# Two blocks at 256 tokens: another order of the attention slots, forget sums in one matmul, and transposed hidden units in both feed-forwards

## The chip, the cores and the metric

The kernel runs on one NeuronCore of a Trainium2 chip. The metric is the device time of one execution in microseconds (us); lower is better. Engines are named as in the profile: PE is TensorE, PEld its weight loads, DVE VectorE, ACT ScalarE, POOL GpSimd and SP SyncE.

## The reference

Two transformer blocks run one after the other on x (256 tokens, 1,024 channels, float32).

```python
# first block
u = rms_norm(h, g_mix); z = u @ w_in
y_a = sliding_window_attention(q_a, k_a, v_a, sinks) @ w_br_swa   # 8 heads of 64, 2 key heads
y_b = forgetting_attention(q_b, k_b, v_b, f_b + b_forget) @ w_br_fox  # scores + c[q] - c[k], c = cumsum(log_sigmoid(f))
h = h + (gates[0] * y_a + gates[1] * y_b) @ w_mix_out
h = h + square(relu(rms_norm(h, g_mlp) @ w_ff1)) @ w_ff2          # 4,096 hidden units
h = h + sigmoid(rms_norm(h, g_ple) @ w_ple_gate) * (p @ w_ple_proj)
y = rms_norm(h, g_final)
# second block, on y, modulated by silu(c) @ w_ada + b_ada
# selected-key attention (8 heads), retention (4 heads), gates, w_out, then
x = x + gate2 * ((silu(h2 @ w_ffn_gate) * (h2 @ w_ffn_up)) @ w_ffn_down)   # 2,816 hidden units
out = rms_norm(x, final_norm_w)
```

## The kernel before

**Weights as units.** Every weight matrix comes through one stream of units of 128 x 1,024 values (two contraction tiles of 128 by 512 columns, or for the down projections one contraction tile by two halves of 512). SP loads a unit into one of the slots of `raw`. ACT copies it to `w_hi` as float32r (a rounded upper half), and DVE subtracts to get `w_lo` (the lower half). `w_hi` and `w_lo` have 4 slots (`SPLIT`), so ACT may write unit u only when PE has used unit u - 4, and both engines run 3 units ahead of PE (`AHEAD`; 2 in the gated feed-forward). A product is three matmuls (`mm3`, L1460): hi x hi, hi x lo, lo x hi.

**A unit on PE.** `unit_pair` (L1466) keeps 128 rows of the activations stationary and moves 512 weight columns: 2 contraction tiles x 2 tiles of rows x 3 = 12 matmuls of 512 columns, with a weight load each. `unit_wide` (L1487) does the same for the down projections.

**The attention slots.** Loop `for n in range(20)` in each engine's program. In slot n, PE does the unit of gate weights 20 + n, the scores of head n, the transposes of the probabilities of head n - 2 (`head_pt`) and the output product of head n - 3 (`head_pv`). Heads 0 to 7 are the sliding-window ones, 8 to 15 the forgetting ones. For a forgetting head each of the two score matmuls is followed by one that adds the cumulative sums (`cum`, 256 columns, picked by the table `pick`, L1601). The other two engines have their order written out:

```python
# ACT, slot n                           # DVE, slot n
split_to(u + AHEAD)                     split_to(20 + n + AHEAD)
(gates' tanh where n % 4 == 3)          head_min(n)
head_exp(n)                             head_norm(n - 1)
head_pt(n - 2)                          head_out_lo(n // 2 - 2)   # n even
head_out_hi(n // 2 - 2)   # n even
```

`head_min` (L965) takes the scores from PSUM and leaves them and their minima in SBUF; `head_exp` (L576) needs that; `head_norm` (L975) needs the exponentials; PE's `head_pt` needs the normed probabilities; ACT's `head_pt` (L585) copies the transposed ones; `head_out_hi` (L591) and `head_out_lo` (L984) split the output of a pair of heads out of bank 7, and PE's `head_pv` of the next pair waits for `aT_lo`. The second block's selected-key attention has the same slots at q = 33 to 44 of a loop over 60 units (head q - 17), without sinks, with `head_out_hi` and `head_out_lo` both at q = 37, 39, 41 and 43.

**The squared-ReLU feed-forward.** 8 chunks of 512 hidden units. Per chunk, 4 units of w_ff1 give the hidden units in banks 0 and 1 with tokens on the partitions; ACT applies relu with the norm's rstd as scale (L688) and squares (L691); PE transposes them into banks 2 and 3 (`hidden_T`, 8 transposes, L1502); ACT and DVE split them into `xT_hi`, `xT_lo` (L696, L1113); 4 units of w_ff2 are added to banks 4 to 7 one chunk later. During this loop DVE also sums the modulation (`ada_acc`, L1134), whose weights POOL loads.

**The gated feed-forward.** 11 chunks of 256 hidden units: 4 units that hold 256 gate columns and 256 up columns (banks 0 and 1, one tile of tokens each), tanh on ACT (L862), two products on DVE (L1410, L1412), 4 transposes on PE (`ffn_T`, L1848), the split (L858, L1403), and 2 units of the down projection.

Of the kernel before, what the change touches and what calls it, by code (L numbers as in the profile page):

```python
# [60 lines left out]
def constants():  # L61
# [71 lines left out]
    "relu": "ACT: relu tiles", "squared": "ACT: squared tiles", "hid_T": "PE: banks of transposed hidden units", "hid_hi": "ACT: upper halves",  # L133
# [8 lines left out]
    "ffn_tanh": "ACT: tanh(gate / 2)", "ffn_silu": "DVE: twice silu", "ffn_hid": "DVE: twice the hidden units", "ffn_T": "PE: transposed",  # L142
    "ffn_hi": "ACT: upper halves", "ffn_lo": "DVE: lower halves", "ffn_out": "PE: the output's banks",
# [27 lines left out]
def build(nc, x, p, g_mix, w_in, b_forget, swa_sinks, w_br_swa, w_br_fox, w_mix_out, g_mlp, w_ff1, w_ff2,  # L171
# [86 lines left out]
    with ExitStack() as ctx:  # L258
# [26 lines left out]
        cum = sb("cum", [LO_ROW + HEADS, SEQ], F32R)  # L285
# [23 lines left out]
        nr8 = sm(2)  # L309
        neg_half = sm(8).rearrange("p (k t) -> p k t", t=2)  # L310
# [217 lines left out]
        def _(act):  # L528
# [96 lines left out]
            for c in range(1, 5):  # L625
# [59 lines left out]
            def relu2(j_done):  # L685

                for t in range(TILES):
                    nc.scalar.activation(nat[:, 0, t, :], B[:, t, :], ACT.Relu, scale=rstd[:, 1, t:t + 1]).then_inc(sem("relu"), 1)  # L688
                act.wait_ge(sem("relu"), j_done)
                for t in range(TILES):  # L690
                    nc.scalar.activation(nat[:, 1, t, :], nat[:, 0, t, :], ACT.Square).then_inc(sem("squared"), 1)  # L691

            def hidden_hi(banks=(0, 1)):
                for i in banks:
                    b = 2 + i
                    nc.scalar.activation(xT_hi[:, 2 * i:2 * i + 2, :], B[:, b, :].rearrange("p (k n) -> p k n", k=2),  # L696
                                         ACT.Copy).then_inc(sem("hid_hi"), 1)
# [3 lines left out]
            act.wait_ge(sem("rstd_done"), 2)  # L701
            act.wait_ge(units_used, U_FF + 4)
            relu2(2)
            act.wait_ge(sem("hid_T"), 2)
            hidden_hi()
            with act.Fori(1, FF_CHUNKS) as j:
# [85 lines left out]
            for q in range(60):  # L792
# [27 lines left out]
                if 13 <= q < 21:  # L820
                    i = q - 13
                    act.wait_ge(sem("index_done"), i + 1)
                    if i >= 2:
                        act.wait_ge(sem("index_sum"), i - 1)
                    nc.scalar.activation(prob[:, i % 2, :], B[:, 4 + i % 2, 0:KEYS], ACT.Relu).then_inc(sem("index_relu"), 1)
                if 33 <= q < 41:
                    head_exp(q - 17, False)
                if 35 <= q < 43:
                    head_pt(q - 19)
# [38 lines left out]
            ffn_hi(0, 1)
            with act.Fori(0, (FN_CHUNKS - 1) // 2) as i:
# [23 lines left out]
        def _(dve):  # L893
# [134 lines left out]
            for k in (1, 2, 3):  # L1028
# [7 lines left out]
                if k == 2:  # L1036
                    dve.wait_ge(sem("cum_hi"), 1)
                    low = slice(LO_ROW, LO_ROW + HEADS)
                    nc.vector.tensor_tensor(cum[low, :], B[low, 7, 0:SEQ], cum[low, :].bitcast(F32), ALU.subtract).then_inc(sem("cum_lo"), 1)

            for n in range(2 * HEADS + 4):
                split_to(20 + n + AHEAD)
                if n < HEADS:
# [66 lines left out]
            def hidden_lo(i, count):  # L1110
                    b = 2 + i
                    dve.wait_ge(sem("hid_hi"), count)
                    nc.vector.tensor_tensor(xT_lo[:, 2 * i:2 * i + 2, :], B[:, b, :].rearrange("p (k n) -> p k n", k=2),  # L1113
# [27 lines left out]
            split_to(U_FFE + 3 + AHEAD)  # L1141
            dve.wait_ge(units_used, U_FFE + 4)
            for t in range(TILES):
                add_h(t, 0, 4 + t)
            for t in range(TILES):
                add_h(t, 1, 6 + t)
# [114 lines left out]
            for q in range(60):  # L1261
# [40 lines left out]
                if 33 <= q < 41:  # L1302
                    if q == 33:
                        dve.wait_ge(sem("selected"), 1)
                    head_min(q - 17, selected)
                if 34 <= q < 42:
                    head_norm(q - 18, False)
                if q in (37, 39, 41, 43):
# [603 lines left out]
```

## Time and profile before

| | |
|---|---|
| median of 3 runs | 876.91 us (876.29 to 877.5) |
| the profiled execution | 877.04 us, of which the span is 875.4 us |
| PE busy | 845.4 us (97%), 3,999 matmuls |
| DVE / ACT / POOL busy | 588.8 (67%) / 443.8 (51%) / 52.4 us (6%) |
| chain that ended last | PE 91%, ACT 3%, DVE 2%, issue 2%, DMA 1% |
| mean granted TensorE clock | 0.991 of full |

Busy time is the sum of the instructions' durations without overlap; matmul records overlap each other, so the pace of PE is read from start to start. A slot or a chunk is found by the line numbers. In a timeline, a row "x3" is three instructions merged, and a bracket at its end tells how long the engine sat idle before it and what it waited for.

### The profile page before, as it was taken

Reading aid. Unit: us, or ns where it says so; the run is one execution under the profiler, and the core shown is the slowest. Engines: PE = TensorE matmul, PEld = TensorE weight load, DVE = VectorE, ACT = ScalarE, POOL = GpSimd, SP = SyncE. Lnnn points to the kernel's source line nnn. Section 1 sums busy time; section 2 is a strip of 40 time slices with the busy share of each in tenths; the row PEclk is TensorE's granted clock in tenths of the full one; section 3 lists DMA queues with packets and bytes.
Section 4 is the critical chain, followed back from the end, with each engine's and each line's share of the span. In section 5 each row is a group of like instructions: output and inputs, shape, how many; then the busy total and the mean of one; then the engine's idle time right before and its main releaser. Section 6 shows DMA issues by size and latency. Waiting matters only on the chain.

```text
span 875.4 us, 11575 instructions
## 1 busy us (share of the span) xinstructions
PE 845.4 (97%) x3999; PEld 704.5 (80%) x3999; DVE 588.8 (67%) x902; ACT 443.8 (51%) x693; POOL 52.4 (6%) x67
## 2 busy tenths in 40 slices
PE   6999999999999999997999999999998999999996
PEld 5888888887888888875988887888887788888885
DVE  4756665867788777877766986656675746545555
ACT  6546665456444445567544436544543535434442
POOL 4000000102000000201100000011000000000000
PEclk9999999999999999999899999999999999999999
DMA  8854334688989898541565564545545365665641
GB/s 278 286 170 141 106 118 140 180 336 314 343 318 320 328 323 320 186 146 25 181 203 153 151 194 149 148 143 171 188 114 166 131 213 155 213 189 164 200 136 48
DMA packets 87621, 170.42 MB, mean 195 GB/s; under 512 B 8176, under 2 KB 32984, under 8 KB 87584
## 3 DMA queue, kind: packets, MB, share of 16 engines
q1 hardware_dynamic: 82272, 142.63, 50.7%
q0 software_dynamic: 5312, 27.30, 9.1%
q8 instruction: 22, 0.36, 0.2%
q14 instruction: 15, 0.12, 0.0%
HBM read 168.84 MB, written 1.05 MB: 194 GB/s over the span
## 4 chain that ended last, share of the span: by engine, by line
PE 91%; ACT 3%; DVE 2%; issue 2%; DMA 1%; POOL 0%; SPq 0%; DVEq 0%; POOLq 0%; ACTq 0%
PE B L1462 27%; PE B L1464 27%; PE B L1463 27%; PE B L1502 3%; PE B L1731 1%; ACT w_hi L536 1%; PE B L1521 1%; DMA raw<-in_w_in_dram 1%; PE B L1510 1%; PE B L1599 1%; ACT Z L579 1%; ACT junk L572 1%; PE B L1767 1%; DVE Z L971 1%; PE B L1848 1%
## 5 line engine op out<-in xcount | busy, mean ns | idle before, releaser
L1462 PE MATMUL B<-w_hi,xT_hi 128*128 128x512 f32 (+2 forms) x760 | 301.5, 397 | 1.3 <-DVE w_lo L908 1.3
L1464 PE MATMUL B<-w_hi,xT_lo 128*128 128x512 f32 (+2 forms) x760 | 294.2, 387 | 0.0
L1463 PE MATMUL B<-w_lo,xT_hi 128*128 128x512 f32 (+2 forms) x760 | 293.9, 387 | 0.0
L908 DVE TENSOR_TENSOR w_lo<-raw,w_hi 128x1024 fp32r<-128x1024 f32 (+2 forms) x156 | 186.9, 1210 | 87.8 <-ACT w_hi L536 86.4
L536 ACT ACTIVATE w_hi<-raw 128x1024 fp32r<-128x1024 f32 (+2 forms) x156 | 158.7, 1029 | 94.7 <-PE B L1464 87.9
L1464 PEld LDWEIGHTS B<-w_hi,xT_lo 128*128 128x128 f32 x760 | 144.1, 190 | 29.0
L1462 PEld LDWEIGHTS B<-w_hi,xT_hi 128*128 128x128 f32 x760 | 144.2, 190 | 28.8 <-issue 2.2
L1463 PEld LDWEIGHTS B<-w_lo,xT_hi 128*128 128x128 f32 x760 | 144.2, 190 | 26.7
L1462 PE MATMUL B<-w_hi,sT_hi 128*128 128x512 f32 x328 | 129.6, 395 | 0.0
L1464 PE MATMUL B<-w_hi,sT_lo 128*128 128x512 f32 x328 | 128.0, 390 | 0.0
L1463 PE MATMUL B<-w_lo,sT_hi 128*128 128x512 f32 x328 | 127.7, 389 | 0.0
L1422 DVE TENSOR_TENSOR w_lo<-raw,w_hi 128x1024 fp32r<-128x1024 f32 x60 | 72.2, 1220 | 37.5 <-ACT w_hi L875 37.5
L711 ACT ACTIVATE w_hi<-raw 128x1024 fp32r<-128x1024 f32 x56 | 58.5, 1057 | 53.0 <-PE B L1464 53.0
L1126 DVE TENSOR_TENSOR w_lo<-raw,w_hi 128x1024 fp32r<-128x1024 f32 x56 | 67.3, 1222 | 25.9 <-ACT w_hi L711 24.9
L875 ACT ACTIVATE w_hi<-raw 128x1024 fp32r<-128x1024 f32 x60 | 62.3, 1057 | 42.8 <-PE B L1464 42.8
L1464 PEld LDWEIGHTS B<-w_hi,sT_lo 128*128 128x128 f32 x328 | 61.6, 188 | 13.2
L1463 PEld LDWEIGHTS B<-w_lo,sT_hi 128*128 128x128 f32 x328 | 61.7, 188 | 12.3
L1462 PEld LDWEIGHTS B<-w_hi,sT_hi 128*128 128x128 f32 x328 | 61.6, 188 | 12.3
L1134 DVE SCALAR_TENSOR_TENSOR Z<-Z,small 128x1536 f32<-128x1536 f32 x28 | 50.7, 1811 | 1.1 <-DMA Z<-in_w_ada_dram 1.1
L579 ACT ACTIVATE Z<-Z,small 128x128 f32<-128x128 f32 (+1 forms) x48 | 21.5, 448 | 43.1 <-DVE small L971 43.1
L1410 DVE SCALAR_TENSOR_TENSOR Z<-Z,B 128x512 f32<-128x512 f32 x11 | 7.6, 688 | 40.6 <-ACT Z L862 40.6
L862 ACT ACTIVATE Z<-B 128x512 f32<-128x512 f32 x11 | 6.6, 600 | 48.3 <-PE B L1464 48.3
(205 smaller groups left out, 698.8 us busy)
## 6 DMA issues: line engine op xcount, KB each, us to landing
raw<-in_w_in_dram SPq DMA_DIRECT2D x88, 512.0 KB, 3.7
raw<-in_w_ff_dram SPq DMA_DIRECT2D x64, 512.0 KB, 6.2
Z<-in_w_ada_dram POOLq DMA_DIRECT2D x32, 768.0 KB, 7.6
raw<-in_w_ffn_gate_dram SPq DMA_DIRECT2D x44, 256.0 KB, 3.5
raw<-in_w_ffn_up_dram SPq DMA_DIRECT2D x44, 256.0 KB, 4.1
raw<-in_w_ffn_down_dram SPq DMA_DIRECT2D x20, 512.0 KB, 4.3
raw<-in_w_mix_out_dram SPq DMA_DIRECT2D x8, 512.0 KB, 3.7
raw<-in_w_ple_gate_dram SPq DMA_DIRECT2D x8, 512.0 KB, 4.1
```

What stands on the lines that cost most here:

```text
L536: nc.scalar.activation(w_hi[:, u % SPLIT, :, 0:n], raw[:, st.slot[u], :, 0:n], ACT.Copy).then_inc(hi_done, 1)
L579: last = nc.scalar.activation(prob[:, n % 2, k0:k1], prob[:, n % 2, k0:k1], ACT.Exp, scale=-1.0, bias=rmin[:, n, t:t + 1], accum_out=psum_ ...
L711: nc.scalar.activation(w_hi[:, u % SPLIT, :, :], raw[:, st.slot[u], :, :], ACT.Copy).then_inc(hi_done, 1)
L875: nc.scalar.activation(w_hi[:, u % SPLIT, :, :], raw[:, st.slot[u], :, :], ACT.Copy).then_inc(hi_done, 1)
L908: nc.vector.tensor_tensor(w_lo[:, u % SPLIT, :, 0:n], raw[:, st.slot[u], :, 0:n], w_hi[:, u % SPLIT, :, 0:n].bitcast(F32), ALU.subtract).t ...
L1126: nc.vector.tensor_tensor(w_lo[:, u % SPLIT, :, :], raw[:, st.slot[u], :, :], w_hi[:, u % SPLIT, :, :].bitcast(F32), ALU.subtract).then_in ...
L1134: nc.vector.scalar_tensor_tensor(ada_acc[:, 1536 * q:1536 * (q + 1)], ada_raw[:, q, :], silu_now, ada_acc[:, 1536 * q:1536 * (q + 1)], ALU ...
L1422: nc.vector.tensor_tensor(w_lo[:, u % SPLIT, :, :], raw[:, st.slot[u], :, :], w_hi[:, u % SPLIT, :, :].bitcast(F32), ALU.subtract).then_in ...
L1462: nc.tensor.matmul(bank, xh, wh, start=start, stop=False)
L1463: nc.tensor.matmul(bank, xh, wl, start=False, stop=False)
L1464: return nc.tensor.matmul(bank, xl, wh, start=False, stop=stop)
L1502: m = nc.tensor.transpose(B[:, b, kk * SEQ + t * P:kk * SEQ + (t + 1) * P], src(t, 2 * i + kk), ident)
```

## The change

In both attentions ACT copies the transposed probabilities of head n - 2 before the exponentials of head n. DVE norms head n - 1 before it takes the minima of head n, and splits a pair's output at slot 2m + 5 instead of 2m + 4, between the norm and the minima. In the forgetting heads the cumulative sums are laid out over the 384 key columns and added with one matmul of 384 columns ahead of the two score matmuls.

In both feed-forwards the first product has the weights stationary and the activations moving (`unit_T`): 4 groups of 128 hidden units x 2 contraction tiles x 3 = 24 matmuls of 256 columns, so the hidden units come out on the partitions and `hidden_T` and `ffn_T` are gone. Bank 0 holds the first 256 hidden units of the unit's 512, bank 1 the others. The norm's rstd is applied squared when the output is added (`rstd2`), since it is now along the free axis. ACT starts on bank 0 at a new signal (`first_bank`), half way through the last unit.

```diff
-                    nc.scalar.activation(cum[:, :], B[0:LO_ROW + HEADS, 7, 0:SEQ], ACT.Copy).then_inc(sem("cum_hi"), 1)
+                    nc.scalar.activation(cum[:, :], B[0:LO_ROW + HEADS, 7, 0:KEYS], ACT.Copy).then_inc(sem("cum_hi"), 1)
@@ ACT, attention slots (and in the same way at q = 33 to 44)
+                if 0 <= n - 2 < 16:
+                    head_pt(n - 2)
                 if n < 16:
                     head_exp(n, n < HEADS)
-                if 0 <= n - 2 < 16:
-                    head_pt(n - 2)
                 if 4 <= n < 20 and n % 2 == 0:
                     head_out_hi(n // 2 - 2, n // 2 - 2)
@@ ACT, squared-ReLU feed-forward
+            def relu2(j_done, chunks):
+                for b in range(2):
+                    if b == 0:
+                        act.wait_ge(sem("first_bank"), chunks)
+                    else:
+                        act.wait_ge(units_used, j_done)
+                    nc.scalar.activation(nat[:, 0, b, :], B[:, b, :], ACT.Relu).then_inc(sem("relu"), 1)
@@
-                act.wait_ge(units_used, j * 8 + (U_FFL - 4))
-                relu2(j * 2 + 2)
+                relu2(j * 8 + (U_FFL - 4), j + 1)
+                act.wait_ge(sem("hid_lo"), j * 2)
+                square(j * 2 + 2)
                 for r in range(7, 7 + AHEAD):
                     loop_split(r)
-                act.wait_ge(sem("hid_T"), j * 2 + 1)
-                hidden_hi((0,))
+                hidden_hi(0, j * 2 + 1)
@@ ACT, gated feed-forward
-                    act.wait_ge(units_used, i * 12 + (U_FNL + 6 * half + 4))
+                    act.wait_ge(sem("first_bank"), i * 2 + (FF_CHUNKS + half + 2))
                     ffn_tanh(1 - half)
@@ DVE, attention slots (and in the same way at q = 33 to 44)
                 split_to(20 + n + AHEAD)
+                if 0 <= n - 1 < 16:
+                    head_norm(n - 1, n - 1 < HEADS)
+                if n >= 5 and n % 2 == 1:
+                    head_out_lo((n - 5) // 2, (n - 5) // 2)
                 if n < HEADS:
                     head_min(n, distance, 2.0 ** -(n + 1), nsink[:, n:n + 1])
                 elif n < 16:
                     head_min(n, causal)
-                if 0 <= n - 1 < 16:
-                    head_norm(n - 1, n - 1 < HEADS)
-                if n >= 4 and n % 2 == 0 and n < 20:
-                    head_out_lo(n // 2 - 2, n // 2 - 2)
@@ DVE, end of the squared-ReLU feed-forward
+            dve.wait_ge(sem("rstd_done"), 2)
+            link(nc.vector.tensor_tensor(rstd2, rstd[:, 1, :], rstd[:, 1, :], ALU.mult))
@@ PE
+            def unit_T(u, xh, xl, kt0, banks, first, last, free=None):
+                s = u % SPLIT
+                for i in range(4):
+                    bank, c0 = banks[i // 2], SEQ * (i % 2)
+                    if free is not None and i % 2 == 0:
+                        pe.wait_ge(*free[i // 2])
+                    cols = slice(i * P, (i + 1) * P)
+                    for kk in range(2):
+                        o, xk, xlk = B[:, bank, c0:c0 + SEQ], xh[:, kt0 + kk, :], xl[:, kt0 + kk, :]
+                        nc.tensor.matmul(o, w_hi[:, s, kk, cols], xk, start=first and kk == 0 and i % 2 == 0, stop=False)
+                        nc.tensor.matmul(o, w_hi[:, s, kk, cols], xlk, start=False, stop=False)
+                        m = nc.tensor.matmul(o, w_lo[:, s, kk, cols], xk, start=False, stop=last and kk == 1 and i % 2 == 1)
+                    if last and i == 1:
+                        m.then_inc(sem("first_bank"), 1)
+                m.then_inc(units_used, 1)
@@
+                    if not swa:
+                        nc.tensor.matmul(B[:, 4 + n % 2, 0:KEYS], pick[:, n - HEADS, :], cum[:, :], start=True, stop=False)
                     for t, (k0, k1) in enumerate(TILE_KEYS):
-                        if not swa:
-                            m = nc.tensor.matmul(s, pick[:, n - HEADS, :], cum[:, 0:k1 - k0], start=False, stop=True)
@@
-            pe.wait_ge(sem("squared"), 2)
-            hidden_T()
             with pe.Fori(1, FF_CHUNKS) as j:
                 for r in range(4):
                     pe.wait_ge(lo_done, j * 8 + (U_FFL + r - 7))
-                    unit_pair(U_FFL + r, sT_hi, sT_lo, 2 * r, (0, 1), r == 0, r == 3, 512)
+                    unit_T(U_FFL + r, sT_hi, sT_lo, 2 * r, (0, 1), r == 0, r == 3,
+                           [(sem("relu"), j * 2 - 1), (sem("relu"), j * 2)] if r == 0 else None)
@@
-            pe.wait_ge(sem("ffn_hid"), 1)
-            ffn_T(0)
@@
-                        if e == 4:
-                            pe.wait_ge(sem("ffn_hid"), i * 2 + (half + 2))
-                            ffn_T(1 - half)
```

## Rows read from the trace of the kernel before

**Rows 1.** The page, part 1: busy time, share of the span and instructions of each engine
```profile
PE 845.4 (97%) x3999; PEld 704.5 (80%) x3999; DVE 588.8 (67%) x902; ACT 443.8 (51%) x693; POOL 52.4 (6%) x67
```

**Rows 2.** Timeline of PE, a gated chunk; columns: start us, us, engine, line, operation, out<-in, xcount
```profile
741.22 0.60 PE L1848 MATMUL B<-cst,Z 128*128 128x128 f32 x4
...
744.42 0.39 PE L1462 MATMUL B<-w_hi,xT_hi 128*128 128x512 f32 x1
...
758.03 0.60 PE L1848 MATMUL B<-cst,Z 128*128 128x128 f32 x4
```

**Rows 3.** Timeline of PE, squared-ReLU loop, two passes' transposes
```profile
220.13 1.03 PE L1502 MATMUL B<-cst,nat 128*128 128x128 f32 x8
...
242.79 1.04 PE L1502 MATMUL B<-cst,nat 128*128 128x128 f32 x8
```

**Rows 4.** Timeline of PE, 264-column matmuls of the first chunk
```profile
16.93 0.28 PE L1464 MATMUL B<-w_hi,xT_lo 128*128 128x264 f32 x1
...
19.45 0.28 PE L1464 MATMUL B<-w_hi,xT_lo 128*128 128x264 f32 x1
```

**Rows 5.** Timeline of PE, 72-column matmuls of the second w_in
```profile
431.51 0.28 PE L1462 MATMUL B<-w_hi,xT_hi 128*128 128x72 f32 x1
...
435.75 0.28 PE L1464 MATMUL B<-w_hi,xT_lo 128*128 128x72 f32 x1
```

**Rows 6.** Timeline of PE, ways into the squared-ReLU loop and into the gated loop
```profile
200.08 1.10 PE L1657 MATMUL B<-sT_hi,zero_r 128*128 128x512 f32 x4
...
203.69 0.48 PE L1462 MATMUL B<-w_hi,sT_hi 128*128 128x512 f32 x1
...
691.16 1.10 PE L1857 MATMUL B<-xT_hi,zero_r 128*128 128x512 f32 x4
...
693.87 0.48 PE L1462 MATMUL B<-w_hi,xT_hi 128*128 128x512 f32 x1
```

**Rows 7.** Windows view, 240:380: us, busy PE, PEld, DVE, ACT, POOL, PEclk, DMA, GB/s
```profile
240.00:380.00 140.00, 140.00 (x649) 116.43 (x649) 111.74 (x97) 70.93 (x87) 16.18 (x21) 1.00 0.83 293
```

**Rows 8.** Timeline of ACT, first attention; the last bracket is the idle time before and its releaser
```profile
73.77 1.04 ACT L536 ACTIVATE w_hi<-raw 128x1024 fp32r<-128x1024 f32 x1
...
90.88 0.47 ACT L589 ACTIVATE Z<-B 128x384 f32<-128x384 f32 x1
91.25 0.37 ACT L593 ACTIVATE sT_hi<-B 128x256 fp32r<-128x256 f32 x1
91.51 1.05 ACT L536 ACTIVATE w_hi<-raw 128x1024 fp32r<-128x1024 f32 x1
...
95.98 1.05 ACT L536 ACTIVATE w_hi<-raw 128x1024 fp32r<-128x1024 f32 x1
```

**Rows 9.** Timeline of DVE, the same slots
```profile
89.68 0.15 DVE L978 TENSOR_TENSOR small<-small 128x2 f32<-128x2 f32 x1
...
90.07 0.55 DVE L981 TENSOR_SCALAR Z<-Z,small 128x128 f32<-128x128 f32 x2
91.64 0.42 DVE L986 TENSOR_TENSOR sT_lo<-B,sT_hi 128x256 fp32r<-128x256 f32 x1 [1.03 <-ACT sT_hi L593]
92.59 1.23 DVE L908 TENSOR_TENSOR w_lo<-raw,w_hi 128x1024 fp32r<-128x1024 f32 x1 [0.52 <-ACT w_hi L536]
93.73 0.35 DVE L971 CUSTOM_DVE_ANT_0 Z<-B,cst,small 128x128 f32<-128x128 f32 x1
```

**Rows 10.** Timeline of ACT, selected attention, splits of weight units
```profile
523.80 1.04 ACT L536 ACTIVATE w_hi<-raw 128x1024 fp32r<-128x1024 f32 x1
...
540.31 1.05 ACT L536 ACTIVATE w_hi<-raw 128x1024 fp32r<-128x1024 f32 x1
...
544.48 1.04 ACT L536 ACTIVATE w_hi<-raw 128x1024 fp32r<-128x1024 f32 x1
```

**Rows 11.** Timeline of PE, products of heads' outputs: slot 15, and slot 7 of the second
```profile
138.57 0.60 PE L1521 MATMUL B<-Z 128*128 128x256 f32 x2
...
549.92 0.60 PE L1521 MATMUL B<-Z 128*128 128x256 f32 x2
```

More of the change, by code:

```diff
@@ L131 @@
     "gated": "DVE: branches times their gates", "mixed_done": "DVE: merged halves' tiles",
-    "relu": "ACT: relu tiles", "squared": "ACT: squared tiles", "hid_T": "PE: banks of transposed hidden units", "hid_hi": "ACT: upper halves",
+    "relu": "ACT: relu tiles", "squared": "ACT: squared tiles", "first_bank": "PE: first of the two banks of a chunk of hidden units", "hid_hi": "ACT: upper halves",
     "hid_lo": "DVE: lower halves", "pT_done": "PE: p transposed", "pT_hi": "ACT: upper half", "pT_lo": "DVE: lower half",
@@ L140 @@
     "mod_1": "DVE: columns of the first norm", "mod_2": "DVE: columns of the second norm", "gate_sum": "PE: gates' rows", "gate_b": "ACT: their copies",
-    "ffn_tanh": "ACT: tanh(gate / 2)", "ffn_silu": "DVE: twice silu", "ffn_hid": "DVE: twice the hidden units", "ffn_T": "PE: transposed",
-    "ffn_hi": "ACT: upper halves", "ffn_lo": "DVE: lower halves", "ffn_out": "PE: the output's banks",
+    "ffn_tanh": "ACT: tanh(gate / 2)", "ffn_silu": "DVE: twice silu", "ffn_hid": "DVE: twice the hidden units",     "ffn_hi": "ACT: upper halves", "ffn_lo": "DVE: lower halves", "ffn_out": "PE: the output's banks",
 }
@@ L309, in build @@
         nr8 = sm(2)
+        rstd2 = sm(2)
         neg_half = sm(8).rearrange("p (k t) -> p k t", t=2)
@@ L683, in _, with square, hidden_hi @@
             split_to(U_FF + 1 + AHEAD)
[L685 to L697, printed above, removed]
-            split_to(U_FF + 3 + AHEAD)
[L701 to L705, printed above, removed]
+            def relu2(j_done, chunks):
[5 more added lines that the diff above has]
+                    nc.scalar.activation(nat[:, 0, b, :], B[:, b, :], ACT.Relu).then_inc(sem("relu"), 1)
+            def square(count):
+                for b in range(2):
+                    act.wait_ge(sem("relu"), count - 1 + b)
+                    nc.scalar.activation(nat[:, 1, b, :], nat[:, 0, b, :], ACT.Square).then_inc(sem("squared"), 1)
+            def hidden_hi(b, count):
+                act.wait_ge(sem("squared"), count)
+                nc.scalar.activation(xT_hi[:, 2 * b:2 * b + 2, :], nat[:, 1, b, :].rearrange("p (k n) -> p k n", k=2),
+                                     ACT.Copy).then_inc(sem("hid_hi"), 1)
+            split_to(U_FF + 3 + AHEAD)
+            relu2(U_FF + 4, 1)
+            square(2)
+            hidden_hi(0, 1)
+            hidden_hi(1, 2)
             with act.Fori(1, FF_CHUNKS) as j:
@@ L1301, in _ @@
                     nc.vector.tensor_tensor(selected[:, :], work, causal, ALU.max).then_inc(sem("selected"), 1)
[L1302 to L1305, printed above, removed]
+                if q == 33:
+                    dve.wait_ge(sem("selected"), 1)
                 if 34 <= q < 42:
                     head_norm(q - 18, False)
-                if q in (37, 39, 41, 43):
-                    head_out_lo((q - 37) // 2 + 8, (q - 37) // 2)
+                if q in (38, 40, 42, 44):
+                    head_out_lo((q - 38) // 2 + 8, (q - 38) // 2)
+                if 33 <= q < 41:
+                    head_min(q - 17, selected)
                 if q in (40, 44):
@@ L1427, in _ @@
                         ffn_split(6 * half + q)
-                    ffn_hidden(1 - half, i * 2 + (half + 2))
+                    ffn_hidden(1 - half, i * 2 + (half + 2), i * 12 + (U_FNL + 6 * half + 4))
                     for q in range(4 + FFN_AHEAD, 6 + FFN_AHEAD):
@@ L1564, in _ @@
                     pe.wait_ge(sem("ones"), 1)
-                    nc.tensor.matmul(B[0:LO_ROW + HEADS, 7, 0:P], lf[:, 0, :], upper, start=True, stop=True)
-                    nc.tensor.matmul(B[0:LO_ROW + HEADS, 7, P:SEQ], lf[:, 0, :], ones, start=True, stop=False)
-                    nc.tensor.matmul(B[0:LO_ROW + HEADS, 7, P:SEQ], lf[:, 1, :], upper, start=False, stop=True).then_inc(sem("cum_done"), 1)
+                    for c0 in (0, P):
+                        nc.tensor.matmul(B[0:LO_ROW + HEADS, 7, c0:c0 + P], lf[:, 0, :], upper, start=True, stop=True)
+                    nc.tensor.matmul(B[0:LO_ROW + HEADS, 7, SEQ:KEYS], lf[:, 0, :], ones, start=True, stop=False)
+                    nc.tensor.matmul(B[0:LO_ROW + HEADS, 7, SEQ:KEYS], lf[:, 1, :], upper, start=False, stop=True).then_inc(sem("cum_done"), 1)
             for n in range(2 * HEADS + 4):
@@ L1641, in _ @@
                     transposes((2, 3), half_rows(h, 0), "wt_done")
-            def hidden_T():
-                transposes((2, 3), lambda t, k: nat[:, 1, t, k * P:(k + 1) * P], "hid_T")
             for kp in range(4):
@@ L1649, in _ @@
                 pe.wait_ge(lo_done, u + 1)
-                unit_pair(u, sT_hi, sT_lo, 2 * kp, (0, 1), kp == 0, kp == 3)
+                unit_T(u, sT_hi, sT_lo, 2 * kp, (0, 1), kp == 0, kp == 3)
                 if kp == 0:
@@ L1843, in _ @@
             normed_T((4, 5), h, 1, None)
-            def ffn_T(par):
-                for kk in range(2):
-                    for t in range(TILES):
-                        m = nc.tensor.transpose(B[:, 2 + par, kk * SEQ + t * P:kk * SEQ + (t + 1) * P],
-                                                ffn_hid[:, par, t * 256 + kk * P:t * 256 + (kk + 1) * P], ident)
-                m.then_inc(sem("ffn_T"), 1)
             for kp in range(4):
```

57 lines of the change are left out of this document (25 added, 32 removed).

## The prediction

> **What bounds the kernel.** The profiled execution took 877.04 us, 1.6 us more than its span of 875.4; the median of the runs is 876.91, so a sum made against the profiled execution is lowered by 0.13 at the end. I read the page's busy times first: PE is busy 97% of the span, DVE 67%, ACT 51% [rows 1]. The busy share of PE overstates it, because the records overlap; so I went to its timeline and took the pace from start to start. Between two sets of transposes in the gated feed-forward, 60 matmuls of 512 columns start in 13.61 us, 0.2268 us each [rows 2], without a gap. In the squared-ReLU loop the windows view shows PE busy for 140 of 140 us, with DVE at 111.7, and the DMA at 0.83 of its time [rows 7]. So in both feed-forwards the time is PE's instructions, and only what PE no longer issues counts.
>
> The attentions are different. Row by row, ACT and DVE take turns there: ACT splits a weight unit (91.51), DVE can subtract only then (92.59, after an idle time), takes the minima when that is through (93.73), ACT must have these for its exponentials, copies the transposed probabilities, and only then comes its next split (95.98) [rows 8, 9]. This ring takes 4.47 us, and 0.26 more in slots with `head_out_hi` (91.25 to 91.51). PE's waits there are small, because a slot of PE is about as long as the ring. An instruction moved into the ring therefore lengthens every slot, and one moved out shortens it, even though DVE and ACT are far from full.
>
> **The feed-forwards: what goes.** A pass of the squared-ReLU loop lasts 22.66 us [rows 3], of which 96 matmuls of 0.2268 are 21.77; the 8 transposes and the slower start after them are the other 0.89, and 7 passes have them: 6.2 us. A gated chunk lasts 16.81 us [rows 2], 72 matmuls are 16.33, so 0.48, in 10 chunks: 4.8 us. On the way into each loop PE also waits for the chunk's nonlinearity: the four zeroing matmuls begin at 200.08 and would be through 0.91 later, at 200.99, but the loop begins at 203.69, 2.70 us later; at the gated one it is 692.07 against 693.87, 1.80 us [rows 6]. Both gaps hold a set of transposes. After the change PE may go on when bank 0 is read, and the signal comes half a unit (1.4 us) before the last unit's end, with the zeroing on top: 2.3 us of cover for one or two instructions of 512 columns per partition, where the 1,024-column ones last 1.05 and 1.23 [rows 8, 9]. I take no wait there. Gone in all: 6.2 + 4.8 + 2.7 + 1.8 = 15.5 us.
>
> **The feed-forwards: what comes.** 32 + 44 = 76 units become 24 matmuls of 256 columns instead of 12 of 512: the same columns, but twice the weight loads. No stream of 256 columns stands in the trace. Near it is one of 264: 21 starts in 2.52 us, 0.1200 each [rows 4]. On a line between 264 and 512 columns a column costs 0.00043, so 256 cost 0.1166. The unit goes from 12 x 0.2268 = 2.722 to 24 x 0.1166 = 2.798 us: 0.076 more, 5.8 us over 76 units. The bounds: 72 columns take 0.1116 each (38 starts in 4.24 us [rows 5]), which is what the weight load alone allows; at that pace a unit is 2.678 and the 76 gain 3.3 us. At the full 0.1200 of rows 4 the units cost 12.0 us. I take 5.8, since 264 is 8 columns away and 72 is 184.
> The Trainium skill ("TensorE: Matmul & The Clock Gate", Back-to-back issue gap) gives N/2.4 + 2.5 ns for a warm matmul. The rows show a larger fixed part: 512 columns at the 2.4 GHz level are 213 ns of 227, 264 are 110 of 120. By the page 256 columns would cost 109.2 and 512 215.8, an estimate of 2.4 us for the 76 units where mine is 5.8.
> Relu, squares, tanh, products and splits keep their number and size; they lie beside PE's matmuls, and with the pass at 22.07 us DVE goes from 0.80 to 0.82 of the loop and the DMA from 0.83 to 0.85 [rows 7]. If that cover were gone the weights would come late, and PE would wait at a unit's start. `rstd2` is one instruction of two columns ahead of a wait for PE: nothing. Feed-forwards together: -15.5 + 5.8 = -9.7 us.
>
> **The attention slots.** On ACT the copy of the transposed probabilities leaves the ring: it now runs while DVE works, 0.37 us less (90.88 to 91.25) [rows 8]. On DVE the norm of head n - 1 enters it, between the subtraction and the minima: from its first step at 89.68 to the scaling at 90.07 is 0.39, the scaling lasts 0.55, and a following instruction starts 0.09 before the end of the one ahead (1.23 long, next after 1.14): 0.85 us [rows 9]. A forgetting or selected head has one small step less, 0.66. In odd slots `head_out_lo` enters as well: 0.42 - 0.09 = 0.33 [rows 9]. It used to run at the end of the slot before, beside ACT.
> New ring, window heads: 4.47 - 0.37 + 0.85 = 4.95; 5.21 in even slots from 4 on, 5.28 in odd ones. Other heads: the ring is 4.17 now (540.31 to 544.48) [rows 10], so 4.46 in the first slots, then 4.72 and 4.79.
> And PE can't slip past it: the output product in an odd slot (from 5 on) waits for `head_out_lo` of the same slot, which stands ahead of that slot's minima. So the products follow the ring. First attention, from ACT's split at 73.77 [rows 8]: slots 1 to 3, 3 x 4.95, gives 88.62; 4 to 7, 2 x (5.21 + 5.28), 109.60; slot 8 (norm of a window head) 4.91, 114.51; 9 to 14, 3 x (4.79 + 4.72), 143.04; in slot 15 split 1.08, subtraction 1.14, norm 0.66, `head_out_lo` 0.42: the product starts at 146.34, against 138.57 [rows 11], 7.8 us later. `head_out_lo` of the last pair is a slot later too, just ahead of the units that need it: 0 to 0.4, I take 0.2. Second attention, from 523.80 [rows 10]: 3 x 4.46, then 4.72 + 4.79 + 4.72 and 3.30 give 554.71 against 549.92 [rows 11]: 4.8 us. Together 12.8 us. Bounds: -1.5, if the ring does not hold PE and its small waits go, and 14, if the tail's 0.4 and some latency come on top.
> The forget sums: PE has one matmul and one weight load less per head, at most 0.11 us [rows 5] x 8 = 0.9; but PE waits for the ring in these slots, so 0. The wider copy of the sums comes once, hidden beside a unit. No DMA moves; SP waits for the same subtractions and POOL's queue is untouched.
>
> **The sum.** 877.04 - 9.7 + 12.8 = 880.1 in the profiled execution, 880.0 as a median. About 0.2% (1.8 us) is what a measurement can tell from no change.
>
> **Rivals.**
> B, faster: PE is free of the ring. ScalarE's copy now comes ahead of the exponentials, so PE's next transposes and products find bank 6 free; if the split of a weight unit has run ahead in time, the subtraction is over before the previous exponentials and norm and minima fit before the scores arrive. It decides where DVE's subtraction in a slot starts without a wait for ACT; the row at 92.59 has a wait [rows 9], which speaks against. Then attention gives -1.5 and the time is 877.0 - 9.7 - 1.5 = 865.8, or some 868 if part of the ring holds.
> C, loads set the pace but do not add: 256 columns at 0.1116. Then 880.0 - 9.1 = 870.9. Against it: 264 columns are far from 0.1116.
> D, doubled loads cost the pace of rows 4: 880.0 + 6.2 = 886.2.
> E, the time per matmul beyond its columns (13 ns at 512 columns, 10 at 264 [rows 2, 4]) halves in this stream: 880.0 - 2.9 = 877.1, no change. Nothing in the rows shows it. The formula named above belongs to this case, and by its estimate the time would be 880.0 - 3.4 = 876.6.
> One part of the change does nothing for the time in the forecast and in most rivals: the forget sums in one matmul. Only in B could their 0.9 us be seen.
>
> **Chances.** Forecast 0.58 (own range 877 to 884), B 0.20, C 0.08, D 0.09, E 0.05. The range from 867 to 886 takes in C, most of D and E and the upper part of B. Faster by over 0.2%: B, C and a little of the forecast, 0.30. Slower: most of the forecast and D, 0.55. The rest 0.15.
>
> **What would show it.** Starts of the 256-column matmuls 0.1166 apart; a pass of the squared-ReLU loop of 22.07 us and a gated chunk of 16.33 + 0.30 = 16.63; no transposes and no wait on the way in. ACT's splits in the first attention 4.95, then 5.2 to 5.3 apart, PE waiting for DVE's `sT_lo` in slot 5 for several us and in each odd slot after, and the branch units starting some 8 us later. The prediction is wrong if these splits stay 4.5 to 4.7 apart (then B), or if the starts are 0.112 or 0.120 apart (C, D).

## The result, and the profile after

The changed kernel takes 894.73 us (median of 4 runs, 892.72 to 895.14) against 877.2 us (876.29 to 878.78) for the kernel before: a ratio of 1.019, 95% interval 1.0173 to 1.0207. The forecast was 880.0, with a range of 867 to 886. Slower was right; the size, 17.5 us where 3 were forecast, lies outside the range.

The page of the profiled execution (895.14 us, span 893.4), for the line in [rows 1]:

```profile
span 893.4 us, 13192 instructions
PE 851.8 (95%) x4797; PEld 744.8 (83%) x4797; DVE 590.0 (66%) x903; ACT 445.2 (50%) x693; POOL 52.4 (6%) x67
```

PE has 798 matmuls more and is busy 6.4 us longer, yet its share falls. So most of the new time is idle time, and the waits of PE name it (what waited, for what, us in total, times, the longest):

```profile
PE B L1543 <- DVE sT_lo L990: 15.5, 8, 5.1
PE B L1745 <- DVE rstd_id L1201: 8.5, 2, 4.8
```

The second line was there before. The first is the product of the heads' outputs (`head_pv`) waiting for `head_out_lo`: 0.4 us before, 15.5 now. PE's timeline in the first attention, slots 5 and 6 and then the products of slots 7 to 15, with [rows 11] as their counterpart:

```profile
97.57 1.19 PE L1543 MATMUL B<-Z 128*128 128x256 f32 x2 [5.08 <-DVE sT_lo L990]
...
98.84 0.77 PE L1467 MATMUL B<-w_hi,xT_hi 128*128 128x512 f32 x1
99.41 0.63 PE L1468 MATMUL B<-w_lo,xT_hi 128*128 128x512 f32 x1
99.84 0.63 PE L1469 MATMUL B<-w_hi,xT_lo 128*128 128x512 f32 x1
...
102.93 0.40 PE L1468 MATMUL B<-w_lo,xT_hi 128*128 128x512 f32 x1
103.17 0.39 PE L1469 MATMUL B<-w_hi,xT_lo 128*128 128x512 f32 x1
103.40 0.81 PE L1623 MATMUL B<-Z 128*128 128x128 f32 x4
...
110.47 0.67 PE L1543 MATMUL B<-Z 128*128 128x256 f32 x2 [1.54 <-DVE sT_lo L990]
...
120.69 0.67 PE L1543 MATMUL B<-Z 128*128 128x256 f32 x2 [0.83 <-DVE sT_lo L990]
...
130.96 0.67 PE L1543 MATMUL B<-Z 128*128 128x256 f32 x2 [0.83 <-DVE sT_lo L990]
...
151.49 0.67 PE L1543 MATMUL B<-Z 128*128 128x256 f32 x2 [0.83 <-DVE sT_lo L990]
```

Three things are to be seen. The 5.08 us in slot 5 are the forecast's stall. Behind it the 512-column matmuls start 0.43 us apart in place of 0.23, for most of one unit, and that was not in the forecast. And from then on two slots take 10.27 us (120.69 to 130.96) where the forecast had 9.51. The windows view (us, busy PE, PEld, DVE, ACT, POOL, granted clock, DMA share, GB/s) shows the clock fall:

```profile
92.00:98.00 6.00, 0.92 (x4) 0.71 (x5) 3.48 (x13) 2.75 (x8) 0.00 (x0) 0.81 0.41 102
98.00:103.00 5.00, 5.00 (x15) 3.95 (x15) 2.11 (x7) 2.12 (x6) 0.00 (x0) 0.55 0.33 95
```

The starts 0.43 us apart are 512 columns at 1.2 GHz.

Up to the stall the slots ran as forecast. ACT's splits at the start of slots 4, 5 and 6, where the forecast had 5.21 and 5.28 us between them:

```profile
88.73 1.05 ACT L536 ACTIVATE w_hi<-raw 128x1024 fp32r<-128x1024 f32 x1
...
93.94 1.04 ACT L536 ACTIVATE w_hi<-raw 128x1024 fp32r<-128x1024 f32 x1
...
99.20 1.04 ACT L536 ACTIVATE w_hi<-raw 128x1024 fp32r<-128x1024 f32 x1
```

The next one came 7.63 us later. In the second attention the products of slots 5 and 7 were:

```profile
555.78 0.67 PE L1543 MATMUL B<-Z 128*128 128x256 f32 x2 [4.58 <-DVE sT_lo L990]
...
567.42 0.67 PE L1543 MATMUL B<-Z 128*128 128x256 f32 x2 [1.01 <-DVE sT_lo L990]
```

In the feed-forwards PE's timeline has the ways into both loops, against [rows 6], and the first matmul of two passes of each, against [rows 2, 3]:

```profile
208.04 0.28 PE L1492 MATMUL B<-sT_hi,w_hi 128*128 128x256 f32 x1
...
212.00 0.28 PE L1492 MATMUL B<-sT_hi,w_hi 128*128 128x256 f32 x1
...
214.52 1.09 PE L1676 MATMUL B<-sT_hi,zero_r 128*128 128x512 f32 x4
215.45 0.28 PE L1492 MATMUL B<-sT_hi,w_hi 128*128 128x256 f32 x1
...
237.87 0.28 PE L1492 MATMUL B<-sT_hi,w_hi 128*128 128x256 f32 x1
...
709.39 1.09 PE L1864 MATMUL B<-xT_hi,zero_r 128*128 128x512 f32 x4
710.32 0.28 PE L1492 MATMUL B<-xT_hi,w_hi 128*128 128x256 f32 x1
...
727.30 0.28 PE L1492 MATMUL B<-xT_hi,w_hi 128*128 128x256 f32 x1
```

Both waits on the way in are gone. The 256-column matmuls start 0.1200 apart (33 starts in 3.96 us), not 0.1166. A squared-ReLU pass is 22.42 us (22.66 before), a gated chunk 16.98 (16.81 before: longer).

How late PE is against before at some points of the program, read from the same rows of both traces: +13.3 us at the last product of the first attention, +13.9 at the first matmul of `w_ff1`, +9.9 at the end of the squared-ReLU feed-forward, +9.8 in the second attention before slot 5, +17.9 at its end, +18.0 at the end of the span. So the slots cost 13.3 and 8.1 us and 0.6 more in the units behind the first attention, one of which waits 0.29 us for the last `head_out_lo`. The first feed-forward gives back 3.9, and the second gives nothing.

### The profile page after: what moved, and what is told of

Same layout as the page of the kernel before. It is cut to its first block, busy times and chain, and to the rows that moved or that the text cites. A ratio compares the mean times of both kernels' runs of the same rounds, so it can differ in the third digit from the quotient of the medians.

```text
span 893.4 us, 13192 instructions
## 1 busy us (share of the span) xinstructions
PE 851.8 (95%) x4797; PEld 744.8 (83%) x4797; DVE 590.0 (66%) x903; ACT 445.2 (50%) x693; POOL 52.4 (6%) x67
## 4 chain that ended last, share of the span: by engine, by line
PE 85%; DVE 6%; ACT 5%; issue 2%; DMA 1%; POOL 0%; SPq 0%; DVEq 0%; POOLq 0%; ACTq 0%
PE B L1467 18%; PE B L1468 18%; PE B L1469 18%; PE B L1494 8%; PE B L1493 8%; PE B L1492 8%; DVE w_lo L912 3%; ACT w_hi L536 2%; PE B L1524 2%; PE B L1745 1%; ACT Z L579 1%; DVE Z L975 1%; PE B L1543 1%; DMA raw<-in_w_in_dram 1%; DVE Z L985 1%
## 5 line engine op out<-in xcount | busy, mean ns | idle before, releaser
L1467 PE MATMUL B<-w_hi,xT_hi 128*128 128x512 f32 (+2 forms) x584 | 234.2, 401 | 0.8 <-DVE w_lo L912 0.8
L1468 PE MATMUL B<-w_lo,xT_hi 128*128 128x512 f32 (+2 forms) x584 | 227.0, 389 | 0.0
L1469 PE MATMUL B<-w_hi,xT_lo 128*128 128x512 f32 (+2 forms) x584 | 226.9, 389 | 0.0
L1492 PE MATMUL B<-xT_hi,w_hi 128*128 128x256 f32 x352 | 99.6, 283 | 0.0
L1494 PE MATMUL B<-xT_hi,w_lo 128*128 128x256 f32 x352 | 99.6, 283 | 0.0
L1493 PE MATMUL B<-xT_lo,w_hi 128*128 128x256 f32 x352 | 99.6, 283 | 0.0
L1129 DVE TENSOR_TENSOR w_lo<-raw,w_hi 128x1024 fp32r<-128x1024 f32 x56 | 67.8, 1223 | 21.3 <-ACT w_hi L717 20.4
L1492 PE MATMUL B<-sT_hi,w_hi 128*128 128x256 f32 x256 | 72.5, 283 | 0.0
L1494 PE MATMUL B<-sT_hi,w_lo 128*128 128x256 f32 x256 | 72.4, 283 | 0.0
L1493 PE MATMUL B<-sT_lo,w_hi 128*128 128x256 f32 x256 | 72.4, 283 | 0.0
L1493 PEld LDWEIGHTS B<-xT_lo,w_hi 128*128 128x128 f32 x352 | 67.5, 192 | 0.4
```

Of the source, the lines that this page charges most:

```text
L1129: nc.vector.tensor_tensor(w_lo[:, u % SPLIT, :, :], raw[:, st.slot[u], :, :], w_hi[:, u % SPLIT, :, :].bitcast(F32), ALU.subtract).then_in ...
L1467: nc.tensor.matmul(bank, xh, wh, start=start, stop=False)
L1468: nc.tensor.matmul(bank, xh, wl, start=False, stop=False)
L1469: return nc.tensor.matmul(bank, xl, wh, start=False, stop=stop)
L1492: nc.tensor.matmul(o, w_hi[:, s, kk, cols], xk, start=first and kk == 0 and i % 2 == 0, stop=False)
L1493: nc.tensor.matmul(o, w_hi[:, s, kk, cols], xlk, start=False, stop=False)
```

## The experiments

**The slots put back, and the slots alone.** The first run takes back both orders in both attentions and keeps the rest; the second does the new orders to the kernel before and nothing else.

```diff
 ACT, both attentions              DVE, both attentions
-head_pt(n - 2)                   -head_norm(n - 1)
 head_exp(n)                      -head_out_lo(...)   # n odd
+head_pt(n - 2)                    head_min(n)
                                  +head_norm(n - 1)
                                  +head_out_lo(...)   # n even
```

> The changed kernel with the slots of both attentions in their old order on ScalarE and VectorE; the forget sums in one matmul and both feed-forwards with stationary weights stay. Theory (the loss of the changed kernel lies in the slots alone): its trace puts the squared-ReLU stage at 3.4 us less than before and the gated one within 0.4 us of before, so 877.2 - 3.4 + 0.4 - 0.5 for the forget sums = about 873.7 us. Rival (256-column matmuls or the forget sums carry the loss, and the slots only show it): it stays at 885 us or more. Second rival (the old slots were only as good as they were because the forget sums left PE late): 877 to 880.

> The kernel before with nothing but the new order of the slots on ScalarE and VectorE in both attentions. Theory: the changed kernel's 894.7 and the 3.4 us that its feed-forwards give back, so 877.2 + 20.4 = about 897.6 us, with PE idle for some 5 us ahead of the first product of an odd slot of either attention and the next matmuls after it at half the granted clock. My forecast's price for the slots alone was 12.8 us: 890. Rival (the slots cost nothing by themselves): 877 to 881.

Measured: 873.38 us with the old slots, ratio to before 0.9957 (0.994 to 0.9973); 899.22 us for the slots alone, 1.0251 (1.0234 to 1.0268). In the second trace PE's wait is the one of the changed kernel:

```profile
PE B L1521 <- DVE sT_lo L986: 15.4, 8, 5.1
```

Both came out near what their theories expected (873.7 and 897.6), and the slots alone far above the 12.8 us of the forecast. The whole loss is the slots: +21.7 us alone and +21.4 within the change (894.73 less 873.38). The rest of the change is worth -4.1 us.

**Which of the moves.** ScalarE's copy (`head_pt`) alone, the copy and the norm, and the copy and `head_out_lo`:

```diff
 copy_first               out_lo_back                  out_lo_only
 head_min(n)              head_norm(n - 1)             head_out_lo(...)  # odd
 head_norm(n - 1)         head_min(n)                  head_min(n)
 head_out_lo(...) # even  head_out_lo(...)  # even     head_norm(n - 1)
```

> The changed kernel with VectorE's old order in the slots, and only ScalarE's new one: the copy of the transposed probabilities ahead of the exponentials. Theory (the loss comes from what enters the ring on VectorE: the norm and head_out_lo): the ring loses the 0.37 us copy and nothing enters, so PE's own slot holds; like the kernel with both old orders less the small waits of the slots, 871 to 873.5 us. Rival (the copy's place on ScalarE causes the wait, since the copy now waits for transposes that PE issues late and the exponentials stand behind it): 880 to 894.

> The changed kernel with head_out_lo alone in its old place (even slots, behind the minima); the norm stays ahead of the minima. Theory (the ring is longer by the norm, but the product of an odd slot waits for a head_out_lo that was issued a slot ahead, so PE has no wait of 5 us and its clock does not fall; the ring of 4.95 to 5.2 us still outlasts PE's slot of about 4.7): 877 to 885 us, of it some 3 to 5 us per attention from the ring. Rival 1 (head_out_lo is the whole loss; the norm's place is free): 872 to 875. Rival 2 (the norm ahead of the minima is the whole loss): 890 to 895.

> The changed kernel with the norm put back behind the minima; head_out_lo stays ahead of the minima of the odd slot. Theory (the product of an odd slot waits for a head_out_lo of the same slot, so the product follows the ring of ACT and DVE, which with only head_out_lo's 0.33 more and the copy's 0.37 less is no longer than before, some 4.5 us a slot): PE loses a few short waits, no wait of 5 us, 874 to 880 us. Rival 1 (costs add: norm alone is 6.7 us, so head_out_lo alone is the other 14.6): 887 to 889. Rival 2 (the odd slot's wait for head_out_lo is free as long as the norm is not in the ring): 873 to 874.

Measured:

| ahead of the minima on DVE | us | ratio to before (95%) |
|---|---|---|
| nothing (copy_first) | 873.46 | 0.9945 (0.9927 to 0.9963) |
| the norm (out_lo_back) | 880.16 | 1.0033 (1.002 to 1.0045) |
| `head_out_lo` (out_lo_only) | 880.51 | 1.0043 (1.0029 to 1.0057) |
| both (the change) | 894.73 | 1.019 (1.0173 to 1.0207) |

The copy's place on ACT costs nothing and gives nothing (873.38 with both old orders). Norm and `head_out_lo` cost 6.7 and 7.0 us one at a time, and 21.3 together; each difference is uncertain by 1 to 2 us, far less than the gap between 13.7 and 21.3. The last expectation missed slightly: 880.5 lies just above its 874 to 880, and the first rival's 887 to 889, which added the costs, is further off. PE's products of slots 5, 6 and 7 with the norm alone:

```profile
94.81 0.67 PE L1543 MATMUL B<-Z 128*128 128x256 f32 x2 [2.15 <-DVE sT_lo L990]
...
99.26 0.60 PE L1543 MATMUL B<-Z 128*128 128x256 f32 x2
...
104.96 0.67 PE L1543 MATMUL B<-Z 128*128 128x256 f32 x2 [1.14 <-DVE sT_lo L990]
```

and of slots 5, 7, 9 and 11 with `head_out_lo` alone:

```profile
92.89 0.67 PE L1543 MATMUL B<-Z 128*128 128x256 f32 x2 [1.92 <-DVE sT_lo L990]
...
102.58 0.67 PE L1543 MATMUL B<-Z 128*128 128x256 f32 x2 [0.68 <-DVE sT_lo L990]
...
112.15 0.67 PE L1543 MATMUL B<-Z 128*128 128x256 f32 x2 [0.17 <-DVE sT_lo L990]
...
121.76 0.67 PE L1543 MATMUL B<-Z 128*128 128x256 f32 x2 [0.17 <-DVE sT_lo L990]
```

With the norm alone the wait runs out: in the forgetting slots the ring is short enough for PE's own pace of 4.60 us again. With `head_out_lo` alone it never runs out: two slots take 9.61 us (112.15 to 121.76) against 9.20 in copy_first. In neither is there a wait over 2.2 us on this line, and in both the granted clock is 1.00 from 92 to 104 us, the slots behind the first of them. The second attention of the run with the norm alone is different. There the wait was shorter, and the clock fell all the same (the second row is the windows view, with a granted clock of 0.50):

```profile
543.41 0.67 PE L1543 MATMUL B<-Z 128*128 128x256 f32 x2 [1.84 <-DVE sT_lo L990]
```

```profile
544.00:547.30 3.30, 3.30 (x11) 2.63 (x10) 2.19 (x8) 1.17 (x6) 0.00 (x0) 0.50 0.33 70
```

The next product came 6.07 us later (549.48), where the slots around it take 4.4, so 1.6 of the norm's 6.7 us are a slow clock.

**The halved clock.** Sixteen matmuls in the idle time of slot 5:

```diff
+if n == 5:
+    pe.wait_ge(sem("evac"), 6)
+    for _ in range(16):
+        nc.tensor.matmul(B[:, 2, :], zero_r[:, :], xT_hi[:, 0:2, :]..., start=True, stop=True)
 head_pv(k, va_pad, k // 4)
```

> The changed kernel with 16 more matmuls of 512 columns (zero weights, into a bank that is free then) in slot 5 of the first attention, in the 5.1 us in which PE waits for VectorE's head_out_lo; 16 x 0.2268 = 3.6 us fit into that. Theory (the clock was at half in the matmuls behind the wait because PE had been idle): the granted clock stays at full there, the unit of slot 6 takes 2.7 to 3.0 us instead of 4.56, and the time falls by 1.5 to 2.3 us to about 892.7; the second attention keeps its halved stretch. Rival (the clock falls there for a cause other than the idle time): the 0.43 us starts stay and the time stays at 894 to 895.

Measured: 892.1 us, ratio 1.0161 (1.0147 to 1.0174): 2.6 us less than the changed kernel, a little more than the 1.5 to 2.3 expected. The same stretch in the windows view, and the product of slot 7 in PE's timeline:

```profile
98.00:103.00 5.00, 5.00 (x28) 4.23 (x27) 2.76 (x9) 2.60 (x8) 0.00 (x0) 1.00 0.34 96
```

```profile
107.72 0.67 PE L1543 MATMUL B<-Z 128*128 128x256 f32 x2 [1.53 <-DVE sT_lo L990]
```

Work that is of no use makes the kernel faster. From the product of slot 5 (97.17 here) to that of slot 7 it is 10.55 us, and 12.90 in the changed kernel (97.57 to 110.47); the forecast's ring gave 10.49.

**The buffer of the probabilities.** In the even slots of the changed kernel DVE's minima are late. DVE's and ACT's timelines in slot 10:

```profile
125.67 0.29 DVE L975 CUSTOM_DVE_ANT_0 Z<-B,cst 128x128 f32<-128x128 f32 x1 [0.69 <-PE B L1532]
```

```profile
126.35 0.40 ACT L579 ACTIVATE Z<-Z,small 128x128 f32<-128x128 f32 x1 [0.30 <-DVE small L975]
...
127.51 1.05 ACT L536 ACTIVATE w_hi<-raw 128x1024 fp32r<-128x1024 f32 x1
```

L1532 are PE's transposes of head n - 2. The minima of head n go into the buffer that they read, since there are two. So two slots are one closed chain with PE in it: product 120.69, a unit, scores and transposes to 125.67 (4.98 us), minima to 126.35 (0.68), exponentials and `head_out_hi` to the split at 127.51 (1.16), the split until DVE subtracts (1.08), subtraction, norm, `head_out_lo` to the product at 130.96 (2.37): 10.27. A third buffer takes away what that wait is for:

```diff
+prob_c = sb("prob_c", [P, KEYS])        # heads n with n % 3 == 2; prob[:, n % 3] for the others
 def head_min(n, ...):
-    if n >= 2: dve.wait_ge(sem("pt_done"), n - 1)
+    if n >= 3: dve.wait_ge(sem("pt_done"), n - 2)
```

> The changed kernel with a third buffer for the heads' probabilities, so that VectorE's minima of head n wait for the transposes of head n - 3, no longer for those of head n - 2. Theory (in the pairs of slots after the first idle time the ring runs through PE: product of the odd slot, unit, scores, transposes, and only then the next minima, since the buffer is in use till then): a pair of slots shrinks from 10.27 us by the 0.6 us between scores and transposes to about 9.7, 5 pairs in the first attention and 3 in the second, some 4.5 us: 890. Rival (the pair is set by ACT's and DVE's own instructions and something else that I missed, not by the buffer): the pairs stay at 10.27 and the time at 894 to 895.

Measured: 892.75 us, ratio 1.0164 (1.015 to 1.0178). Two slots take 9.83 us here:

```profile
128.87 0.67 PE L1548 MATMUL B<-Z 128*128 128x256 f32 x2 [0.42 <-DVE sT_lo L995]
...
138.69 0.67 PE L1548 MATMUL B<-Z 128*128 128x256 f32 x2 [0.42 <-DVE sT_lo L995]
```

So the buffer is part of it, but 2.0 us and not the 4.5 expected: the chain still goes through PE, one step earlier. In the same trace the minima wait 0.23 us for PE's scores:

```profile
133.39 0.29 DVE L980 CUSTOM_DVE_ANT_0 Z<-B,cst 128x128 f32<-128x128 f32 x1 [0.23 <-PE B L1628]
```

**The pace of narrow matmuls.** Two kernels, profiled once each: the changed kernel with the old slots, in which the matmuls with stationary weights move fewer of the 256 tokens; the rest is not computed, so only their pace is read.

```diff
-o, xk, xlk = B[:, bank, c0:c0 + SEQ], xh[:, kt0 + kk, :], xl[:, kt0 + kk, :]
+o, xk, xlk = B[:, bank, c0:c0 + n], xh[:, kt0 + kk, 0:n], xl[:, kt0 + kk, 0:n]
```

> The changed kernel with both attentions' slots in the old order, where a matmul with stationary weights moves 240 of the 256 columns in the squared-ReLU loop and 192 in the gated loop; the columns left out are not computed. Theory (a matmul of this kind costs its columns at the full clock and 13.4 ns, as 512 columns at 0.2268 and 256 at 0.1200 both do, until the 0.1116 of the 72-column rows, which the weight load sets): 240 columns start 0.1134 apart, 192 start 0.1116 apart. Rival 1 (0.1200 is itself a floor set by the weight load of 128x128 with waits, whatever the columns): 0.1200 in both. Rival 2 (my line through 264 and 512 columns, shifted to 0.1200 at 256): 0.1193 and 0.1172.

> As the kernel with 240 and 192 columns, but with 252 columns of 256 in the squared-ReLU loop and 248 in the gated loop; the columns left out are not computed. With 240 columns the starts were 0.1120 apart, with 256 0.1200. Theory (columns at the full clock and a fixed part, on a floor of 0.112): 252 columns 0.1184 and 248 columns 0.1167, on the slope from the floor to 0.1200. Rival (a step between 240 and 256, flat on both sides, since 264 columns have 0.1200 as well): each of the two is at 0.112 or at 0.120.

First and last of one unbroken stretch each, 240 and 192 columns (74 and 87 intervals):

```profile
203.78 0.27 PE L1492 MATMUL B<-sT_hi,w_hi 128*128 128x240 f32 x1
...
212.07 0.27 PE L1494 MATMUL B<-sT_hi,w_lo 128*128 128x240 f32 x1
...
699.28 0.25 PE L1492 MATMUL B<-xT_hi,w_hi 128*128 128x192 f32 x1
...
708.97 0.27 PE L1492 MATMUL B<-xT_hi,w_hi 128*128 128x192 f32 x1
```

252 and 248 columns (76 and 77 intervals), from the second kernel:

```profile
203.78 0.28 PE L1493 MATMUL B<-sT_lo,w_hi 128*128 128x252 f32 x1
...
212.65 0.28 PE L1494 MATMUL B<-sT_hi,w_lo 128*128 128x252 f32 x1
...
704.83 0.28 PE L1492 MATMUL B<-xT_hi,w_hi 128*128 128x248 f32 x1
...
713.68 0.28 PE L1494 MATMUL B<-xT_hi,w_lo 128*128 128x248 f32 x1
```

That is 0.1120, 0.1114, 0.1167 and 0.1149 us; later passes of the same loops, 95 intervals each, have 0.1116, 0.1114, 0.1166 and 0.1150. There is a floor at about 0.112, which 72, 192 and 240 columns share. From 240 to 252 the 12 columns cost 4.7 to 5.0 ns, 0.4 each as at the full clock; the last 4 to 256 cost 3.3. A floor at 0.1200 is excluded, and so is one step with nothing between. The expected 0.1134, 0.1184 and 0.1167 for 240, 252 and 248 were 1.4 to 1.8 ns too high: the part beyond the columns is 11.6 ns at 248 and 11.7 at 252, 13.3 at 256, 10.0 at 264 and 13.5 at 512. It is not one constant, and what makes it differ stays open.

**The gated feed-forward put back,** in the kernel with the copy first. Its units keep tiles of tokens stationary again, and PE transposes.

```diff
-unit_T(U_FN + kp, xT_hi, xT_lo, 2 * kp, (0, 1), kp == 0, kp == 3)
+unit_pair(U_FN + kp, xT_hi, xT_lo, 2 * kp, (0, 1), kp == 0, kp == 3)
...
+pe.wait_ge(sem("ffn_hid"), 1)
+ffn_T(0)
...
-unit_T(u, xT_hi, xT_lo, 2 * e, (0, 1), e == 0, e == 3, ...)
+unit_pair(u, xT_hi, xT_lo, 2 * e, (0, 1), e == 0, e == 3, 512)
...
+if e == 4:
+    pe.wait_ge(sem("ffn_hid"), i * 2 + (half + 2))
+    ffn_T(1 - half)
```

> As copy_first (the changed kernel with VectorE's slots in the old order), and with the gated feed-forward as before (pairs of tiles, transposes); the squared-ReLU one keeps its stationary weights. Theory (a 256-column matmul costs 0.1200, so the 44 gated units cost 7.0 us more where the transposes and the way in give back 6.6): 0.4 us less than copy_first, 873.0 within 1. Rival (the gated change pays as I forecast, 4.0 gained less 2.6 lost by the 0.0034 more per matmul, or more): 875 to 876.5.

Measured: 872.53 us, ratio to before 0.994 (0.9927 to 0.9954). It agrees with 0.4 us less than copy_first, though a difference that small is within the intervals; a gated part worth the 4.0 - 2.6 us of the rival would have given 875. With the copy first, the forget sums in one matmul and stationary weights in the squared-ReLU part alone, this kernel has the lowest median of the study, below both that the case began with, though its interval overlaps those of copy_first and of the old slots.

## Why the prediction was wrong

**What held.** PE is what bounds the feed-forwards. The transposes and the two waits on the way in are gone as forecast, with no wait in their place. The ring of ACT and DVE bounds the slots, `head_out_lo` binds PE to it, and slot 5 has the stall. ACT's splits came 5.21 and 5.26 us apart where 5.21 and 5.28 were forecast, and the product of slot 5 came at 97.57 where the ring gives 97.32 (slot 4 at 88.62, one slot of 5.21, and 3.49 from the split to the product).

**First and second attention: +12.8 forecast, 21.4 measured** (13.3 and 8.1). The step that failed is the sum over slots 6 to 15, in which the ring was ACT and DVE alone. The product of slot 15 came at 151.49, 5.1 us after the forecast 146.34. Of these:
- 0.25 us were there in slot 5.
- 2.4 us lie between the products of slots 5 and 7 (12.90, not 10.49). It is the halved clock, and the sixteen matmuls took it away. The forecast had no term for it, although the trace of the kernel before has the like: a wait of 4.84 us ahead of the product at 414.58 (L1731), with the granted clock at 0.50 from 412.2 to 419.0.
- 2.5 us lie in the four pairs of slots after that (41.02, not 38.53). The forecast said that the products follow the ring and did not follow them back: once PE waits for the ring, the ring's next minima wait for what PE issues behind that product. The third buffer took 1.5 of the 2.5 away (39.49 us for the four pairs) and showed PE's scores as next in line; that these account for the other 1.0 was not tested.
The second attention had the same: a wait of 4.58 us in its slot 5, a halved clock after it, and 8.1 us where 4.8 were forecast. From the product of slot 5 to that of slot 7 it was 11.64 us (555.78 to 567.42), where the ring gives 9.51, so 2.1 of the 3.3 us lie there; no run kept the clock up in this attention. The last `head_out_lo` of the first attention, put at 0.2 us, cost some 0.6 in the units behind it.

**The feed-forwards: -9.7 forecast, about -3.8 read from the two traces (-3.9 and +0.1).** The step that failed is the 0.1166 read off a line between 264 and 512 columns. At 0.1200 the 76 units cost 12.0 us, the upper bound that I had written down and given 0.09 (rival D), and 15.5 less 12.0 is what is left. The line assumed that the part beyond the columns falls evenly from 13.5 ns at 512 to 10.0 at 264 and goes on falling; at 256 it is 13.3. For the gated part this turns the sign of a chunk: 96 x 0.1200 + 24 x 0.2268 = 16.96 us, against 16.81 before, so the 10 chunks lose what the way in gains. The Trainium skill ("TensorE: Matmul & The Clock Gate", Back-to-back issue gap) gives 109.2 ns for 256 columns by its formula for an isolated matmul; the rows have 120.0, and 111 is the least that any width had in a stream of weight units here, so rival E fell too. E had also been priced wrongly: half of a fixed part of 10 ns in 1,824 matmuls is 9 us and not 2.9, about what rival C had.

**The forget sums: 0 forecast.** From the product of slot 8 to that of slot 15 PE takes 32.20 us with the old slots and one matmul, and 32.44 in the kernel before with two: 0.24 us less, against the 0.9 that was put as the most. With the new slots it is some 0.3 too: the changed kernel reaches the zeroing (214.52) 0.30 us later than the slots alone, and its 4 units of `w_ff1` ahead of it cost 0.63 more. The zero of the forecast was near, but its reason, that PE waits for the ring, is not borne out: the little that the sums give is there with either order. They were not run alone.

**Rival B** had it that PE would be free of the ring. With ACT's copy ahead of the exponentials and without the two moves on DVE it is: copy_first has no wait for `sT_lo` at all. That is worth nothing that can be measured, since the old slots had only 0.4 us of it.

The terms, in the profiled execution: 880.1 + 6.2 (the pace) + 5.3 and 3.3 (the attentions) = 894.9, against 895.14.

## What to carry to other kernels

Where an engine's instruction is moved ahead of another, draw the whole cycle with the waits on both sides, those for buffers too: a ring of two engines becomes one of three as soon as the third waits in it, and two moves that cost 7 us each cost 21 together. Behind an idle time of PE of several us, count one unit at the slow clock; one of 1.84 us was enough once, so look at the granted clock of every trace. Take the pace of a matmul of a new width at the nearest measured row, not on a line through two rows that come from different streams, and work out the sign of each place of use at that pace: here it paid in one feed-forward and not in the other.

## What was not expected of the hardware

- The granted clock was 0.50 from 95.7 to 102.5 us in the first attention, where PE had 5.08 us without a matmul, and from 556.5 to 559.9 in the second, behind 4.58 us without one; 512 columns then start 0.43 us apart, as at 1.2 GHz. Sixteen matmuls on zeros kept the clock up. After 2.15 and 1.92 us in the first attention of the runs with one move it stayed up, but after 1.84 us in the second attention of one of them it fell. Nor is idle time needed: in the kernel before, 72-column matmuls without a gap went from 0.11 us apart [rows 5] to 0.21, at a granted clock of 0.50 from 436.1 to 439.4:

```profile
436.10 0.41 PE L1464 MATMUL B<-w_hi,xT_lo 128*128 128x72 f32 x1
436.31 0.41 PE L1462 MATMUL B<-w_hi,xT_hi 128*128 128x72 f32 x1
436.53 0.41 PE L1463 MATMUL B<-w_lo,xT_hi 128*128 128x72 f32 x1
```

  What tells these cases apart no run here settles.
- A 128 x 128 float32r weight load with its matmul took 0.111 to 0.112 us from 72 to 240 columns in the streams of weight units. From there it rises: 0.1149 at 248, 0.1167 at 252, 0.1200 at 256, and again 0.1200 at 264.
- The product of a pair writes the other half of the bank that `head_out_lo` reads, so the wait guards no bytes but the bank. The Trainium skill ("PSUM — Partial Sum Buffer", PSUM bank collisions raise a hardware error) says that accesses of two engines to the same bank in the same group of 32 partitions collide, whether they touch the same bytes or not; no run here shows it, and a kernel without that wait was not tried on the chip.
